# A two-block transformer layer on one Trainium2 core: memory keys and values projected first, and attention maxima ahead of the preceding step's normalising

## What is computed

```
kv_me = rmsnorm_2(mem, norm_mem[l]) @ w_mem_kv[l]
k_me = kv_me[..., :MEM_W].reshape(B_, M_, MEM_HEADS, MEM_HEAD_DIM)
v_me = kv_me[..., MEM_W:].reshape(B_, M_, MEM_HEADS, MEM_HEAD_DIM)
o_me = memory_attention(q_me.reshape(B_, S_, MEM_HEADS, MEM_HEAD_DIM), k_me, v_me)
```

## Time and profile before

| what | value |
|---|---|
| median of 3 runs | 1713.09 us (1712.9 to 1713.82) |
| profiled execution | 1714.07 us |
| its span, first to last instruction | 1712.3 us |
| TensorE matmul busy | 1593.6 us (93%) |
| VectorE, ScalarE, GpSimd busy | 544.3, 442.7, 7.3 us |
| mean granted TensorE clock | 0.981 |
| read from HBM | 522.72 MB |

### The profile page before, as it was taken

The page is one execution under the profiler, slowest core; times in us unless marked ns, Lnnn a source line. Parts: engine busy times, 40 slices in busy tenths (PEclk is TensorE's granted clock), DMA queues, the critical chain, the costliest instruction groups (busy, mean ns, idle before and its releaser), DMA issues.

```text
span 1712.3 us, 23738 instructions
## 1 busy us (share of the span) xinstructions
PE 1593.6 (93%) x10016; PEld 982.3 (57%) x10016; DVE 544.3 (32%) x1090; ACT 442.7 (26%) x854; POOL 7.3 (0%) x16
## 2 busy tenths in 40 slices
PE   5999999999999999999999999998799989899997
PEld 3786676443333343334333433333399978789997
DVE  3754513110101011010101010101355564468863
ACT  3434523010101010011101100000445552455642
POOL 0000000000000000000000000000000100000000
PEclk9999998999999999999999999999899989999999
DMA  9325853999999999999999999999634524425420
GB/s 394 150 91 210 330 173 111 422 437 433 429 429 436 433 429 432 435 432 429 432 435 432 429 433 435 431 429 433 294 123 149 185 99 148 148 99 197 170 102 25
DMA packets 27432, 524.79 MB, mean 306 GB/s; under 512 B 2931, under 2 KB 7027, under 8 KB 7492
## 3 DMA queue, kind: packets, MB, share of 16 engines
q1 hardware_dynamic: 24368, 519.06, 72.9%
q10 hardware_dynamic: 2484, 3.19, 0.7%
q0 software_dynamic: 512, 1.57, 0.4%
HBM read 522.72 MB, written 1.08 MB: 306 GB/s over the span
## 4 chain that ended last, share of the span: by engine, by line
PE 58%; DMA 34%; DVE 4%; ACT 2%; issue 1%; SPq 0%; ACTq 0%; DVEq 0%
PE ps L584 57%; DMA ring<-in_w_down 33%; DMA ring<-in_first 1%; DMA arena<-in_ctxT 1%; DVE mx L1710 1%; PE ps L1065 0%; ACT arena L1306 0%; PE ps L712 0%; DVE arena L1612 0%; DVE nrm L1609 0%; ACT w_high L1435 0%; DVE ring_r L1630 0%; DVE hx_lo L1637 0%; DVE arena L1643 0%; DVE arena L1940 0%
## 5 line engine op out<-in xcount | busy, mean ns | idle before, releaser
L584 PE MATMUL ps<-ring,arena 128*64 128x512 f32 (+1 forms) x3872 | 722.6, 534 | 45.6 <-DMA ring<-in_w_down 31.1
L584 PEld LDWEIGHTS ps<-ring,arena 128*64 128x64 f32 (+1 forms) x3872 | 240.9, 133 | 479.0 <-issue 403.9
L584 PE MATMUL ps<-arena_r,w_high 128*128 128x256 f32 x1840 | 340.4, 287 | 10.2 <-DVE arena_r L1920 9.4
L584 PEld LDWEIGHTS ps<-arena_r,w_high 128*128 128x128 f32 x1840 | 290.6, 194 | 15.1 <-issue 12.8
L584 PE MATMUL ps<-arena 64*128 64x256 f32 (+7 forms) x1780 | 264.9, 382 | 6.3 <-DVE arena L1823 1.6
L584 PE MATMUL ps<-arena_r,ring_r 128*128 128x256 f32 x920 | 262.1, 285 | 0.0
L1847 DVE TENSOR_SCALAR arena<-ps 128x512 f32<-128x512 f32 x32 | 22.1, 692 | 716.2 <-PE ps L584 716.2
L584 PEld LDWEIGHTS ps<-arena 64*128 64x128 f32 (+3 forms) x1780 | 169.1, 178 | 111.5 <-issue 98.1
L584 PEld LDWEIGHTS ps<-arena_r,ring_r 128*128 128x128 f32 x920 | 178.6, 194 | 0.0
L1894 DVE TENSOR_TENSOR ring_r<-ring,w_high 128x1024 fp32r<-128x1024 f32 x120 | 142.0, 1221 | 86.0 <-ACT w_high L1435 86.0
L1435 ACT ACTIVATE w_high<-ring 128x1024 fp32r<-128x1024 f32 x120 | 120.6, 1050 | 26.4 <-PE ps L584 26.4
(11 more groups left out here) (205 smaller groups left out, 1061.9 us busy)
## 6 DMA issues: line engine op xcount, KB each, us to landing
ring<-in_w_gate_up SPq DMA_DIRECT2D x64, 4096.0 KB, 20.8
ring<-in_w_down SPq DMA_DIRECT2D x32, 4096.0 KB, 19.7
ring<-in_second SPq DMA_DIRECT2D x32, 2048.0 KB, 8.1
ring<-in_first SPq DMA_DIRECT2D x19, 2048.0 KB, 9.5
ring<-in_first SPq DMA_DIRECT2D x3, 1024.0 KB, 4.9
ring<-in_second SPq DMA_DIRECT2D x2, 1024.0 KB, 5.2
small<-in_small ACTq DMA_DIRECT2D x1, 1024.5 KB, 8.1
arena<-in_xT SPq DMA_DIRECT2D x1, 1024.0 KB, 7.9
```

The lines of the kernel that those rows point to most:

```text
L584: return nc.tensor.matmul(out_, lhsT, rhs, start=start, stop=stop, **kw)
```

## The change

1. The memory tile is the first transfer. All of the memory's keys' weights come as one unit into slot 4 behind the context, the values' weights as unit 3, and the fourth `w_mod` unit as unit 4, into slot 0. The units of w_in come next.
2. ScalarE squares the memory first, TensorE sums it first; VectorE normalises it after `cs`. TensorE makes both key jobs, then three modulation rows, value job, fourth modulation row, value job. Results go to `k_me1` and `v_me1`; GpSimd copies them to `k_me` and `v_me` after the first attention loop (`kv_moved`).
3. The modulation of x and context is done in two halves: chunks 0 to 3 after three modulation rows, chunks 4 to 7 after the fourth.
4. The modulation rows of the attention loop move from steps 8 to 15 to steps 5 to 12. No memory jobs are left there or after the norm.
5. In both loops VectorE takes the maxima of step a before it normalises step a-1. ScalarE copies the transposes of a-1 after the exponentials of a, in the first loop from step 5 on, in the second in every step.

The core of the diff:

```diff
@@ -101,18 +103,18 @@
-FIRST = [blocks("w_mod", 512 * u, 512) for u in range(4)]
+KEYS = blocks("w_mem_kv_2", 0, 512)
+FIRST = [blocks("w_mod", 512 * u, 512) for u in range(3)]
+U_KV = len(FIRST)
+FIRST += [blocks("w_mem_kv_2", 512, 512), blocks("w_mod", 512 * 3, 512)]
...
 FIRST += [blocks("w_in", 512 * u, 512) for u in range(4)] + [blocks("w_in", 2048, 256)]
-U_KV = len(FIRST)
-FIRST += [blocks("w_mem_kv_2", 0, 256), blocks("w_mem_kv_2", 512, 512)]
...
 FIRST += [blocks("w_out", 512 * u, 512) for u in range(2)]
-U_KV2 = len(FIRST)
-FIRST += [blocks("w_mem_kv_2", 256, 256)]
 U_MOE = len(FIRST)
+U_MOD = (0, 1, 2, U_KV + 1) + tuple(range(U_MOD2, U_OUT))
@@ -399,18 +401,10 @@
-        ADA_STEP = 5
-        KV_STEP = len(JOBS) - EARLY
-        ADA_STEP = KV_STEP + 3
-        KV_JOBS = (("k", 0, U_KV, 0), ("v", 0, U_KV + 1, 1), ("v", 1, U_KV + 1, 0), ("k", 1, U_KV2, 6))
-        def kv_at(a):
-            return a - KV_STEP if KV_STEP <= a < ADA_STEP else None
+        ADA_STEP = len(JOBS) - EARLY
+        KV_JOBS = (("k", 0), ("k", 1), ("v", 0), ("v", 1))
@@ -480,10 +474,9 @@
-        freed = [(ada_mm, n + 1) for n in range(4)]
+        freed = [(ada_mm, n + 1) for n in range(3)] + [(kv_mm, 4), (ada_mm, 4)]
         freed += [(proj_mm, 1 + max(LAST_JOB[p] for p in range(N_PARTS1) if PARTS1[p][0] == U_IN + u)) for u in range(5)]
-        freed += [(kv_mm, 1), (kv_mm, 3)]
-        freed += [(ada_mm, n + 1) for n in range(4, 12)] + [(out_mm, 2), (out_mm, 4), (kv_mm, 4)]
+        freed += [(ada_mm, n + 1) for n in range(4, 12)] + [(out_mm, 2), (out_mm, 4)]
@@ -515,11 +508,11 @@
+            sp.dma_start(memT, io["memT"]).then_inc(mem_in, 16)
...
             sp.dma_start(hx[:, :, T:2 * T], io["ctxT"]).then_inc(ctx_in, 16)
+            sp.dma_start(ring[:, SLOT_KEYS, :], keys).then_inc(slot_full[SLOT_KEYS], 16)
             for u, src in enumerate(first):
-                if u == U_IN + 4:
-                    sp.dma_start(memT, io["memT"]).then_inc(mem_in, 16)
@@ -573,6 +566,10 @@
             nc.gpsimd.memset(b_gu, 0.0).then_inc(bgu_zero, 1)
+            pool.wait_ge(proj_mm, len(JOBS))
+            pool.wait_ge(kv_act, 4)
+            nc.gpsimd.tensor_copy(k_me, k_me1).then_inc(kv_moved, 1)
+            nc.gpsimd.tensor_copy(v_me, v_me1).then_inc(kv_moved, 1)
@@ -590,11 +587,12 @@
             pe.wait_ge(ones_set, 2)
-            sum_squares(NORM1, sq, 7, 2 * T)
+            sum_squares(NORM_MEM, sq_m, 7, T)
+            sum_squares(NORM1, sq, 6, 2 * T)
             def ada_rows(n, bank):
-                u = n if n < 4 else U_MOD2 + n - 4
+                u = U_MOD[n]
@@ -611,10 +609,36 @@
+            def memory_job(n):
+                kind, i = KV_JOBS[n]
+                at = SLOT_KEYS if kind == "k" else U_KV % RING1
+                w = slot(at, KC)
+                if n == 0:
+                    pe.wait_ge(mem_set, KC)
+                if n >= 2:
+                    pe.wait_ge(kv_act, n - 1)
+                pe.wait_ge(slot_full[at], 16)
+                if kind == "k":
+                    for c in range(2):
+                        for k in range(KC):
+                            last = mm(ps[:, i, T * c:T * c + T], w[:, k, P * (2 * i + c):P * (2 * i + c) + P], memT[:, k, :],
+                                      k == 0, k == KC - 1)
+                else:
+                    for k in range(KC):
+                        last = mm(ps[:, i, :], memT[:, k, P * i:P * i + P], w[:, k, :], k == 0, k == KC - 1)
+                last.then_inc(kv_mm, 1)
+            memory_job(0)
+            memory_job(1)
             pe.wait_ge(cs_set, 1)
-            for n in range(4):
+            for n in range(3):
...
                 ada_turn(n, COL_BANKS[n])
+            memory_job(2)
+            ada_rows(3, 5)
+            ada_turn(3, COL_BANKS[3])
+            memory_job(3)
@@ -625,6 +649,8 @@
                 name, i = JOBS[n]
+                if n < 2:
+                    pe.wait_ge(kv_act, n + 3)
@@ -671,10 +697,6 @@
                            buckets[0:33, 512 * g:512 * g + 512], True, True).then_inc(brow_mm, 1)
-                if MEM_JOB < n <= MEM_JOB + 4:
-                    k = 2 * (n - MEM_JOB - 1)
-                    pe.wait_ge(brow_set, 2)
-                    sum_squares(NORM_MEM, sq_m, 7, T, k, k + 2)
@@ -733,39 +755,17 @@
-            def memory_job(n):
-                kind, i, u, bank = KV_JOBS[n]
-                w = slot(u % RING1, KC) if kind == "v" else ring[:, u % RING1, 0:2048].rearrange("p (k n) -> p k n", k=KC)
-                if n == 0:
-                    pe.wait_ge(mem_set, KC)
-                    pe.wait_ge(proj_dve, len(ROPED))
-                    pe.wait_ge(proj_act, len(COPIED))
-                if n == 2:
-                    pe.wait_ge(kv_act, 1)
-                pe.wait_ge(slot_full[u % RING1], filled(u))
-                if kind == "k":
-                    for c in range(2):
-                        for k in range(KC):
-                            last = mm(ps[:, bank, T * c:T * c + T], w[:, k, P * c:P * c + P], memT[:, k, :],
-                                      k == 0, k == KC - 1)
-                else:
-                    for k in range(KC):
-                        last = mm(ps[:, bank, :], memT[:, k, P * i:P * i + P], w[:, k, :], k == 0, k == KC - 1)
-                last.then_inc(kv_mm, 1)
...
                     project(EARLY + a)
-                if kv_at(a) is not None:
-                    memory_job(kv_at(a))
...
                     if a == ADA_STEP:
-                        pe.wait_ge(kv_act, 3)
+                        pe.wait_ge(proj_dve, len(ROPED))
+                        pe.wait_ge(proj_act, len(COPIED))
@@ -793,7 +793,6 @@
             sum_squares(NORM2, sq2, 2, T)
-            memory_job(3)
@@ -1037,6 +1035,8 @@
                 b = a % 2
+                if a == 0:
+                    pe.wait_ge(kv_moved, 2)
@@ -1190,18 +1190,31 @@
             load_table(ACT.Sqrt)
+            act.wait_ge(mem_in, 16)
+            for k in range(KC):
+                square(NORM_MEM, k, sq_m[:, k % 2], memT[:, k])
+            root(NORM_MEM, 7)
...
                 if k >= 2:
-                    act.wait_ge(sq_used, k - 1)
+                    act.wait_ge(sq_used, KC * NORM1 + k - 1)
...
             load_table(ACT.Sqrt)
-            act.wait_ge(sq_used, KC)
-            A(rope1, ps[:, 7, :], ACT.Sqrt, bias=eps[:, 0:1], scale=1.0 / D).then_inc(root_set, 1)
+            act.wait_ge(sq_used, KC * (NORM1 + 1))
+            A(rope1, ps[:, 6, :], ACT.Sqrt, bias=eps[:, 0:1], scale=1.0 / D).then_inc(root_set, 1)
+            def copy_memory(n):
+                act.wait_ge(kv_mm, n + 1)
+                kind, i = KV_JOBS[n]
+                if kind == "k":
+                    A(k_me1[:, 2 * i:2 * i + 2], ps[:, i, :].rearrange("p (a b) -> p a b", a=2), ACT.Copy).then_inc(kv_act, 1)
+                else:
+                    A(v_me1[:, i], ps[:, i, :], ACT.Copy).then_inc(kv_act, 1)
@@ -1209,7 +1222,9 @@
-            for n in range(4):
+            copy_memory(0)
+            copy_memory(1)
+            for n in range(3):
@@ -1220,10 +1235,19 @@
-            split_hi1(0)
-            for k in range(KC):
+            def normed_hi(k):
...
+            for k in range(KC // 2):
+                normed_hi(k)
+            copy_memory(2)
+            ada_copy(3, 5)
+            split_hi1(0)
+            for k in range(KC // 2, KC):
+                normed_hi(k)
+            copy_memory(3)
@@ -1284,19 +1302,7 @@
-            def copy_memory(n):
-                act.wait_ge(kv_mm, n + 1)
-                kind, i, _, bank = KV_JOBS[n]
-                if kind == "k":
-                    A(k_me[:, 2 * i:2 * i + 2], ps[:, bank, :].rearrange("p (a b) -> p a b", a=2),
-                      ACT.Copy).then_inc(kv_act, 1)
-                else:
-                    A(v_me[:, i], ps[:, bank, :], ACT.Copy).then_inc(kv_act, 1)
             for a in range(N_AT + 2):
-                if ADA_STEP <= a <= N_AT:
-                    copy_turn("p", a - 1)
@@ -1309,6 +1315,8 @@
                               bias=negm[:, b, c:c + 1]).then_inc(sinkexp_set, 1)
+                if ADA_STEP <= a <= N_AT:
+                    copy_turn("p", a - 1)
@@ -1316,8 +1324,6 @@
                     copy_job(EARLY + a)
-                if kv_at(a) is not None:
-                    copy_memory(kv_at(a))
@@ -1474,6 +1479,7 @@
             load_table(ACT.Exp)
+            act.wait_ge(kv_moved, 2)
@@ -1492,8 +1498,6 @@
             for a in range(N_C + 2):
-                if c_filler(a) is None and 1 <= a <= N_C:
-                    copy_turn_c(a - 1)
@@ -1511,8 +1515,8 @@
                     copy_c(c_filler(a))
-                    if a >= 1:
-                        copy_turn_c(a - 1)
+                if 1 <= a <= N_C:
+                    copy_turn_c(a - 1)
@@ -1595,35 +1599,41 @@
-            dve.wait_ge(root_set, 1)
+            rinv = nrm[:, 0]
+            def inverse_rms(norm):
```

(58 more changed lines are left out.)

34 lines of the change are left out of this document (14 added, 20 removed).

## The result

The changed kernel takes 1778.2 us (median of 4, 1776.66 to 1779.13), the one before 1713.45 in the same job: a ratio of 1.0376, with a 95% interval of 1.0358 to 1.0393. The forecast was 1770 with a range of 1737 to 1788, slower. The profiled execution has a span of 1776.7 us against 1712.3, so 64.4 us are to be found.

| landmark on TensorE | before | after | growth since the last one |
|---|---|---|---|
| first 512-wide key projection | 57.10 | 83.46 | +26.4 |
| scores of step 0, first loop | 108.35 | 131.30 | -3.4 |
| output projection behind that loop | 226.91 | 282.47 | +32.6 |
| first projection ahead of the second loop | 1238.81 | 1295.34 | +1.0 |
| end of the span | 1712.3 | 1776.7 | +7.9 |

A forecast was written before the change was run, and what follows sets the result against it. TensorE was taken to bound the kernel, with the weight stream in the 32 experts. 24.3 (opening less ones-products) + 12.1 + 18 + 2.9 = 57 on 1714.07 gave 1771, as a median 1770 us; range 1737 to 1788.

The forecast's parts named there:

- The opening: Before the first loop: memory products delay the full key projections from 57.1 to 85 us, +27.9.
- The slow beginning: Opening, first key products: after TensorE's idle the array starts at a low clock again, charged at 2.8 us.
- the last chain: End of the opening, last value product to full projections: copy, splits, modulations, low parts and rope, 13.2 us unhidden.
- Faster: Rival: the opening's products run in its gaps and the new order is free; 1708 us, chance 0.05.
- Ones-products: Stretch behind the opening, bound by TensorE: four pairs of ones-products of 0.9 us each go, -3.6.
- First loop: First attention loop: +12.1 us at full clock from waits and moved work, plus +18 for the lowered clock.
- The wait of 3.2 a step: First loop, steps without a projection between scores and transposes: TensorE idles 3.2 us for maxima (2.2) and normalising.
- A row step: First-loop step with a modulation row: 8.5 us at full clock, 6.4 without a row; 1.6 charged for the clock.
- Full clock: Rival: everything as forecast, but the granted clock stays up in the first loop; 1752 us, chance 0.2.
- The order costs nothing: Rival: VectorE normalises before the scores end, so only the opening's 24.3 remains; 1724 us, chance 0.08.
- Router: Behind the first loop: hiding half the product's wait (some 2) against clock loss up to 3; taken as 0.
- Second loop: Five steps without a projection wait for maxima and normalising, about 0.5 or 0.7 each: +2.9, bounds 0 and 6.

The follow-up runs named there:

- n1: The changed kernel with VectorE's normalising of the memory moved ahead of its wait for the conditioning vector's sigmoid: 1770.88 us, 1.0325 against the kernel before.
- f1: The changed kernel with 14 unused identity products ahead of the transposes in steps 6 to 15 of the first loop: 1763.43 us, 1.0289 against before.
- b1: The kernel before with VectorE's maxima put ahead of normalising in the first loop, ScalarE as it was: 1750.43 us, 1.0212 against before.
- s1: The changed kernel with VectorE's and ScalarE's orders undone in both loops, leaving the move of the memory work: 1729.48 us, 1.0088 against before.
- u1: The changed kernel with VectorE's order undone in the first loop only: 1748.33 us, 1.0194 against before.
- k2: The changed kernel with 7.0 us of unused products behind the output projection, where the fourth memory product stood: 1781.88 us, 1.0395 against before.
- c4: The kernel before with the second loop's value product of step a-2 ahead of the transposes of step a-1: 1715.23 us, 1.0007 against before.
- u2: The changed kernel with VectorE's order undone in the second loop only: 1769.53 us, 1.0318 against before.
- c2: The changed kernel with modulation rows (first loop) and value products (second loop) put ahead of the transposes, VectorE's new order kept: 1745.42 us, 1.0179 against before.
- g1: The kernel before with unused identity products ahead of the transposes in steps 14, 15 and 17 of the second loop: 1712.20 us, 0.9984 against before.
- s2: s1 with the memory's normalising also ahead of VectorE's wait for the sigmoid: 1723.85 us, 1.0059 against before.
- k1: The changed kernel with 14.0 us of unused products behind the output projection, where the fourth memory product stood: 1787.69 us, 1.0427 against before.

## Why the prediction was right, step by step

- **The opening, +27.9, measured +26.4.** The order on VectorE was as said: reciprocal at 24.97 behind `cs`, key products from 30.06 (said: 30.5). It is worth 8.1 of the 26.4, by n1; the other 18.3 stay there, with 28 us of memory products ahead of the projections. The slow beginning charged at 2.8 was 2.1. The DMA queue stood empty as said (share 0.02 from 40 to 45), and the last chain of 13.2 us was 13.1 (70.4 to 83.46). The rival *Faster* needed the memory normalised by 20 and the products under way by 22. n1 has it at 21.0 and starts them at 24.19, behind the sums of squares; until the last value product ends, near 62, TensorE then idles only four times for 0.40 us. The products found no gaps to lie in.
- **Ones-products, -3.6, measured -3.4.**
- **First loop, +12.1 at full clock and +18 for the clock, together +30.1, measured +32.6.** The wait of 3.2 a step was 3.08 in steps 9 and 11 to 15, and 3.2 to 4.1 in the others from step 5 on. f1 separates the two parts: 15.2 at full clock, 17.4 for the clock. A row step was to take 10.1 and took 9.5 to 10.5, 11.2 with the head norm, a plain one 8.0 and took 7.9 to 8.2. Steps 5 to 15 together come out within 2 us of the sum, and steps 0 to 4 grew by 5.4 instead of 4.0, since the clock fell behind the wait of step 4 too. *Full clock* and *The order costs nothing* fall by f1 and b1. (In the latter's sum three steps of 5.6 are 12.8 less than 29.6, not 12.3.)
- **ScalarE's copies** I did not price at all. That did no harm to the sum, since under the whole change TensorE hardly waits for them; with VectorE's order undone they cost 12 us (s1 against u1). This was luck: the prediction never asked what they would cost.
- **Router, 0, measured +1.0.** In these two executions a cancellation: 7 us of product went, and the slow stretch became about 14 us longer. k2 shows that the product was not quite free there. That length varies by itself (c4), so the +1.0 is luck within some 3 us.
- **Second loop, +2.9, measured +7.9. This is the term that was mis-sized.** I had said 0.5 for each of three one-head steps and 0.7 for each of two two-head ones. The one-head steps came out right: their waits went from 3.34 to 5.11, +1.8 (the 2.62 of the shuffle only moved a step forward). The two-head ones did not: from 0 to 1.92 and from 1.04 to 2.79, 1.8 each. The waits thus grew by 5.4. The loop grew by 9.1 (1.2 came back behind it), and for the remaining 3.7 the slow clock is the one cause seen, 24 us instead of 10, which I charged in the first loop and not here. f1 and k2 agree: they have the same five waits (9.8 and 9.9) with the clock down for 17 us, and this loop is 2.6 and 2.3 us shorter there. u2 shows that the order is all of it: without it the loop takes 223.7 us, before 223.9.

The Trainium skill ("TensorE: Matmul & The Clock Gate", HAM oscillation) describes a loop, there with waits for transfers, that loses the clock anew in each pass; here no transfer is waited for, but the mean of 0.83 in eight windows in a row agrees, and f1 is the counterproof, worth 15 us. Without that term the forecast would have been 1752.

## What to carry to other kernels

Ask of every reordering on a helper engine which instruction of the bounding engine stands next in line for the piece that became later, and whether work without that dependence can be put ahead of it; here the moved rows (c2) gave back 27 of the 33 us that the first loop had lost, and together with the value product moved in the second loop 34 of all 65. A wait of 3.08 us made its step 4.3 us longer (9.93 against 5.59), so price a repeated wait with the clock that follows it. And work taken out of a loop gives back only what was not cover: of 21 us moved, 8 came back (s1).

## What was not expected of the hardware

- Products that compute nothing made two kernels faster: by 15 us in the changed one, and by 2.7 us (0.16%) in the kernel before.
- The slow stretch at the router lasts 10 us in the profiled executions of before and g1 and 17 in that of c4, three kernels with the same code up to there. In the change and five of its relatives it lasts 24 us (u2, n1, s1, s2, f1 beside it), in k1 and k2 20.5, in b1 14, and in u1 and c2 it falls into two, of 10 and 7.
- A wait need not bring the clock down: step 5 waits 1.83 us in s1 and in s2, and only in s2 did the clock fall behind it.
